# Stick-breaking attention: scores kept instead of computed twice

## The chip, the cores and the metric

The kernel runs on one core of a Trainium2 chip. The metric is the device time of one execution in microseconds. Before the change the median of three runs is 3508.5 us (3507.38 to 3514.27).

## The reference

The program is a two-block network on 512 tokens with 1024 features. The first block has two layers. Each layer projects the normalised input, runs five attention branches, gates and merges them. The change touches one of these branches, stick-breaking attention, with 4 heads of 64:

```
z = einsum('bqhd,bshd->bhqs', q, k) * scale            # scores
strict = s < t                                         # key strictly before the query
log_keep = where(strict, log_sigmoid(-z), 0)
later = cumsum(log_keep, keys, reverse=True) - log_keep
a = where(strict, exp(log_sigmoid(z) + later), 0)
out = einsum('bhqs,bshd->bqhd', a, v)
```

Since log_sigmoid(z) = z + log_sigmoid(-z), the exponent is z plus the inclusive suffix sum of log_keep. That is how both kernels compute it.

## The kernel before

**Layout.** Keys lie on partitions, queries on the free axis. For a head, key block b (128 keys) meets only the queries from block b on, so the four tiles of a head have 512, 384, 256 and 128 columns. A matmul in plain fp32 appears in the trace as two MATMUL instructions.

**Work for one head, `sb_tensor`, `sb_scalar` and `sb_vector` (lines 1655 to 1805).** `scores(hd)` on TensorE writes the four score tiles into PSUM. `negated(hd)` on VectorE copies them with the sign turned into `lk` (line 1769) and writes -|z| into `wt` (line 1773). `logs(hd)` on ScalarE replaces `wt` by log(1 + exp(wt)) (lines 1731 and 1734). `kept(hd)` on VectorE makes log_sigmoid(-z) from both in `lk` (line 1781) and multiplies its diagonal 128 columns by a 0/1 mask (line 1785). `weights(hd)` on TensorE builds the exponent in a PSUM bank: the score product again, the additive mask on the diagonal block (an identity product with `before_add`), a triangular product `from_here` for the suffix sum inside the block, and products with ones for the later blocks. `weights(hd)` on ScalarE takes the exponential from PSUM into `wt` (line 1742). `weigh(hd)` on TensorE multiplies by the values, and `gated(hd)` on VectorE multiplies the output by its gate (line 1793).

**Order.** Each engine runs its instructions in the order in which they are written; semaphores join the engines. On TensorE a round is `scores(hd + 1)`, filler, `weights(hd)`, filler, `weigh(hd)`. I call these filler A and filler B. On VectorE it was `negated(hd + 1)`, `kept(hd + 1)`, two filler items, `gated(hd)`. Two sets of `lk` and `wt` alternate between heads; one lies in an arena called `arena_even` in the trace, the other in `merged`.

**Filler.** In this branch the filler is the computation of the adaptive-norm modulations for the second block (`ada_tensor`, line 841). Each item on TensorE first claims one of two spare PSUM banks for `ada_columns` and turns the row of the item before it into columns (line 852, two columns wide), and then multiplies four streamed weight chunks by the conditioning (line 867). A claim waits until the former owner of the bank is drained. The columns always take the same one of the two banks, so an item's claim waits for VectorE's write of the columns of the item before (`ada_vector`, line 899, output `mods`). ScalarE copies the row (line 886).

**Elsewhere.** All projections use a high and a low part of the weights (lines 318 to 320). The weights stream from HBM in chunks of 512 KB through five slots on SyncE's queue.

Of the kernel before, what the change touches and what calls it, by code (L numbers as in the profile page):

```python
# [11 lines left out]
ALU = mybir.AluOpType  # L12
ACT = mybir.ActivationFunctionType
# [300 lines left out]
def mm(g, out, a, b, start, stop):  # L314
    pe = g.pe
    if not isinstance(a, Split):
        return pe.matmul(out, a, b, start=start, stop=stop)  # L317
    pe.matmul(out, a.high, b.high, start=start, stop=False)  # L318
    pe.matmul(out, a.high, b.low, start=False, stop=False)  # L319
    return pe.matmul(out, a.low, b.high, start=False, stop=stop)  # L320
# [1334 lines left out]
def sb_tensor(g, l, turn, opening):  # L1655

    pe, S, t, h = g.pe, g.event, g.t.sb, g.t.h
    key = lambda *a: ("sb", l) + a
    for j in range(2):
        for n in "qk":  # L1660
            project(g, key(n, j), turn, COL["sb_" + n][j * P:(j + 1) * P], (l,), h)
        if j == 0:
            fill_tensor(g)
    values_tensor(g, key("v"), turn, COL["sb_v"], (l,), h)
    ready = [S("zeroed").at("queries"), S("drained").at(key("v"))]
    ready += [S("drained").at(key(n, j)) for n in "qk" for j in range(2)]

    def scores(hd):
        j = hd // 2
        for b in range(QT):  # L1670
            i = g.claim(key("z", hd, b), turn.next(1))
            for m in g.after(pe, *ready):
                pe.wait_ge(*m)
            mm(g, g.banks(i)[:, 0:SEQ - b * P], t.k[:, j, b * P:(b + 1) * P], t.q[:, hd, b * P:SEQ], True,
               True).then_inc(*S("scored").up(pe, key(hd, b)))

    def weights(hd):
        j, lk = hd // 2, t.lk[hd % 2]
        for b in range(QT):
            n = SEQ - b * P  # L1680
            bank = g.banks(g.claim(key("w", hd, b), turn.next(1)))
            mm(g, bank[:, 0:n], t.k[:, j, b * P:(b + 1) * P], t.q[:, hd, b * P:SEQ], True, False)
            mm(g, bank[:, 0:P], g.ident, g.c.before_add, False, False)
            for m in g.after(pe, S("kept").at((l, hd))):
                pe.wait_ge(*m)
            done = mm(g, bank[:, 0:n], g.c.from_here, lk[b], False, b == QT - 1)
            for b2 in range(b + 1, QT):
                done = mm(g, bank[:, (b2 - b) * P:n], g.ones, lk[b2], False, b2 == QT - 1)
            done.then_inc(*S("scored").up(pe, key("w", hd, b)))

    def weigh(hd):
        wt = t.wt[hd % 2]
        i = g.claim(key("o", hd), turn.next(1))
        for m in g.after(pe, S("drained").at(key("w", hd, QT - 1))):
            pe.wait_ge(*m)
        for q in range(QT):
            for b in range(q + 1):
                done = mm(g, g.banks(i)[:, q * HD:(q + 1) * HD], wt[b][:, (q - b) * P:(q - b + 1) * P],
                          t.v[:, b, hd * HD:(hd + 1) * HD], b == 0, b == q)
        done.then_inc(*S("weighed").up(pe, key(hd)))  # L1700

    scores(0)
    fill_tensor(g)
    for hd in range(HEADS):
        if hd + 1 < HEADS:
            scores(hd + 1)
        fill_tensor(g)
        weights(hd)
        fill_tensor(g)
        weigh(hd)  # L1710


def sb_scalar(g, l, opening):
    act, S, t = g.act, g.event, g.t.sb
    key = lambda *a: ("sb", l) + a
    for j in range(2):
        g.weights.round(key("q", j))
        pair_scalar(g, key("q", j), pair_of(t.q, j), SCALE)
        g.weights.round(key("k", j))
        if j == 0:  # L1720
            fill_scalar(g)
    g.weights.round(key("v"))
    copy_scalar(g, key("v"), t.v[:, :, :].rearrange("p t c -> p (t c)"), g.bank(key("v"), 2))
    act.preload_act_table_set("natural_log_exp_and_others")

    def logs(hd):
        wt = t.wt[hd % 2]
        for b in range(QT):
            for m in g.after(act, S("stick").at((l, hd, b))):
                act.wait_ge(*m)  # L1730
            act.activation(wt[b], wt[b], ACT.Exp).then_inc(*S("stick_exp").up(act))
            for m in g.after(act):
                act.wait_ge(*m)
            act.activation(wt[b], wt[b], ACT.Ln, bias=1.0).then_inc(*S("stick_log").up(act, (l, hd, b)))

    def weights(hd):
        wt = t.wt[hd % 2]
        for b in range(QT):
            k = key("w", hd, b)
            for m in g.after(act, S("scored").at(k), S("kept").at((l, hd))):  # L1740
                act.wait_ge(*m)
            act.activation(wt[b], g.bank(k)[:, 0:SEQ - b * P], ACT.Exp).then_inc(*S("drained").up(act, k))

    logs(0)
    fill_scalar(g)
    for hd in range(HEADS):
        if hd + 1 < HEADS:
            logs(hd + 1)
        fill_scalar(g)
        weights(hd)  # L1750
        fill_scalar(g)


def sb_vector(g, l, opening):
    dve, S, t = g.dve, g.event, g.t.sb
    key = lambda *a: ("sb", l) + a
    for j in range(2):
        pair_vector(g, key("k", j), t.k[:, j, :])
        if j == 0:
            fill_vector(g)  # L1760

    def negated(hd):
        lk, wt = t.lk[hd % 2], t.wt[hd % 2]
        before = [S("weighed").at(key(hd - 2))] if hd > 1 else []
        for b in range(QT):
            k = key("z", hd, b)
            for m in g.after(dve, S("scored").at(key(hd, b)), *before):
                dve.wait_ge(*m)
            dve.tensor_scalar(lk[b], g.bank(k)[:, 0:SEQ - b * P], -1.0, None, ALU.mult).then_inc(
                *S("drained").up(dve, k))  # L1770
            for m in g.after(dve):
                dve.wait_ge(*m)
            dve.scalar_tensor_tensor(wt[b], lk[b], -1.0, lk[b], ALU.mult, ALU.min).then_inc(
                *S("stick").up(dve, (l, hd, b)))

    def kept(hd):
        lk, wt = t.lk[hd % 2], t.wt[hd % 2]
        for b in range(QT):
            for m in g.after(dve, S("stick_log").at((l, hd, b))):
                dve.wait_ge(*m)  # L1780
            dve.scalar_tensor_tensor(lk[b], lk[b], 0.0, wt[b], ALU.min, ALU.subtract).then_inc(
                *S("stick").up(dve))
            for m in g.after(dve):
                dve.wait_ge(*m)
            dve.tensor_tensor(lk[b][:, 0:P], lk[b][:, 0:P], g.c.before01, ALU.mult).then_inc(
                *S("kept").up(dve, (l, hd) if b == QT - 1 else None))

    def gated(hd):
        k = key("o", hd)
        y = g.t.gate[:, 2, :].rearrange("p (t c) -> p t c", t=QT)[:, :, hd * HD:(hd + 1) * HD]  # L1790
        for m in g.after(dve, S("weighed").at(key(hd))):
            dve.wait_ge(*m)
        dve.tensor_tensor(y, g.bank(k)[:, 0:QT * HD].rearrange("p (t c) -> p t c", t=QT), y, ALU.mult).then_inc(
            *S("drained").up(dve, k))

    negated(0)
    kept(0)
    fill_vector(g)
    for hd in range(HEADS):
        if hd + 1 < HEADS:  # L1800
            negated(hd + 1)
            kept(hd + 1)
        fill_vector(g, 2)
        gated(hd)
# [2513 lines left out]
def pack_constants():  # L4318
# [9 lines left out]
    causal[:, SEQ - P:] = np.where(j <= i, 0.0, NEG)  # L4328
    at["causal"] = first.const(causal)

    at["before01"] = first.const((i < j) * 1.0)
    at["before_add"] = first.const(np.where(i < j, 0.0, NEG))
    at["from_here"] = first.const((i >= j) * 1.0)

# [87 lines left out]
def name_constants(at, common, first):  # L4422
    c, s = Names(), Names()
    c.causal = first[:, at["causal"]:at["causal"] + SEQ]
    sq = lambda t, n: t[:, at[n]:at[n] + P]
    c.before01, c.before_add, c.from_here = (sq(first, n) for n in ("before01", "before_add", "from_here"))
    c.perm64, c.perm32 = sq(first, "perm64"), sq(first, "perm32")
    col = lambda t, n, w=1: t[:, at[n]:at[n] + w]
    c.inv64, c.inv32, c.sign64, c.sign32 = (col(first, n) for n in ("inv64", "inv32", "sign64", "sign32"))
# [31 lines left out]
def tiles(of, **more):  # L4461
    return namedtuple("Tiles", list(of) + list(more))(*of.values(), *more.values())


def layout_first(g, at, t_common, first, st):
# [35 lines left out]
        with ExitStack() as s2:  # L4501
            t.merged_split = g.pair("merged", [P, KT, SEQ], s2)
    heads = [("k", [P, 2, SEQ]), ("v", [P, QT, BR])]
    pieces = [(f"{n}{b}", [P, SEQ - b * P]) for n in ("lk", "wt") for b in range(QT)]
    of = carve(even, heads + pieces)
    sets = (of, carve(t.merged[:, :, :].rearrange("p k n -> p (k n)"), pieces))
    t.sb = tiles(of, q=t.q_even, lk=[[o[f"lk{b}"] for b in range(QT)] for o in sets], wt=[[o[f"wt{b}"] for b in range(QT)] for o in sets])
    of = carve(odd, heads + [("c_kv", [P, 1, SEQ]), ("c_n", [P, 1, SEQ]), ("qi", [P, SEQ]), ("ki", [P, SEQ]),
                                ("work", [P, 2, SEQ])] + [(f"drop{i}", [P, (i + 1) * P]) for i in range(1, QT - 1)])
    t.dsa = tiles(of, q=t.q_odd, drop=[None] + [of[f"drop{i}"] for i in range(1, QT - 1)] + [of["c_n"][:, 0, :]])  # L4510
# [245 lines left out]
```

## Time and profile before

| what | value |
|---|---|
| median of three runs | 3508.5 us |
| profiled execution, own time | 3506.41 us |
| its span | 3505.1 us |
| TensorE busy | 3292.2 us, 94% |
| VectorE busy | 1721.1 us, 49% |
| ScalarE busy | 1313.9 us, 37% |
| mean granted TensorE clock | 0.973 of full |

Rows name engines as PE (TensorE matmul), PEld (its weight load), DVE (VectorE), ACT (ScalarE), POOL (GpSimd), SP (SyncE). The granted clock is given in parts of full speed; it has two levels, 1.0 and 0.5. A stretch with a value between them spent part of its time at each. In a row of the timeline, matmuls that overlap are merged, so the time that one of them takes from the next is the difference of two starts. A bracket at the end of a row is the idle time of the engine before it and who ended it.

### The profile page before, as it was taken

What the parts mean: (1) busy time and instruction counts of PE and PEld (TensorE: products, weight loads), DVE (VectorE), ACT (ScalarE), POOL (GpSimd) and SP (SyncE); (2) the same over time, 40 slices, a digit from 0 to 9 for tenths busy, and PEclk for the clock granted to TensorE, in tenths of its full rate; (3) what the DMA queues carried; (4) which work ended last, traced back from release to release, by engine and by line L of the source; (5) the groups of instructions that cost most, each with busy time, mean ns of one, the idle gap of its engine ahead of it and who ended that gap; (6) DMA issues with size and microseconds to landing.
All of it is one profiled execution on the core that took longest, in us unless ns stands there. A gap on an engine that the chain in (4) does not pass through costs nothing.

```text
span 3505.1 us, 44707 instructions
## 1 busy us (share of the span) xinstructions
PE 3292.2 (94%) x17128; PEld 2630.5 (75%) x17128; DVE 1721.1 (49%) x3172; ACT 1313.9 (37%) x2278; POOL 1056.1 (30%) x513
## 2 busy tenths in 40 slices
PE   8999999999999998999898899999999988889999
PEld 6677777777867776777786677888988556668877
DVE  5348345423138635532798655222565655543234
ACT  4333334333333333333423433222443455533332
POOL 3123122234303222124336432232553000034443
PEclk9999899999999999999999999999999999999999
DMA  5532121132562122124222001122332100022222
GB/s 183 182 136 81 40 81 65 53 101 99 180 221 77 47 70 84 41 70 141 67 67 67 1 31 61 61 67 67 112 117 82 40 35 1 4 71 91 99 96 79
DMA packets 87479, 286.41 MB, mean 82 GB/s; under 512 B 9697, under 2 KB 20321, under 8 KB 86497
## 3 DMA queue, kind: packets, MB, share of 16 engines
q1 hardware_dynamic: 85968, 272.67, 22.9%
q10 hardware_dynamic: 1296, 10.88, 0.8%
q8 instruction: 135, 2.21, 0.3%
q14 instruction: 80, 0.65, 0.1%
HBM read 279.32 MB, written 4.19 MB: 81 GB/s over the span
## 4 chain that ended last, share of the span: by engine, by line
PE 54%; DVE 7%; ACT 3%; issue 2%; POOL 0%; DMA 0%; DVEq 0%; ACTq 0%; POOLq 0%
PE psum L318 14%; PE psum L319 14%; PE psum L320 14%; PE psum L317 9%; PE psum L3768 1%; DVE mla_cols L3857 1%; PE psum L3756 1%; PE psum L1192 1%; DVE padded L2806 0%; DVE h_low L582 0%; DVE ml_weights L3209 0%; PE psum L3734 0%; DVE squares L511 0%; ACT weights_high L395 0%; ACT mla_probs L3813 0%
## 5 line engine op out<-in xcount | busy, mean ns | idle before, releaser
L413 POOL TENSOR_TENSOR weights_low<-weights_loaded,weights_high 128x1024 fp32r<-128x1024 f32 (+3 forms) x456 | 958.6, 2102 | 2362.7 <-ACT weights_high L395 2277.6
L318 PE MATMUL psum<-h_high,weights_high 128*128 128x512 f32 (+1 forms) x2384 | 900.4, 378 | 45.5 <-DVE h_low L582 21.2
L319 PE MATMUL psum<-h_low,weights_high 128*128 128x512 f32 (+1 forms) x2384 | 882.6, 370 | 0.0
L320 PE MATMUL psum<-h_high,weights_low 128*128 128x512 f32 (+1 forms) x2384 | 881.7, 370 | 0.0
L395 ACT CAST weights_high<-weights_loaded 128x1024 fp32r<-128x1024 f32 (+3 forms) x456 | 422.0, 926 | 472.7 <-PE psum L320 398.3
L318 PEld LDWEIGHTS psum<-h_high,weights_high 128*128 128x128 f32 x2384 | 456.1, 191 | 134.4 <-issue 35.7
L319 PEld LDWEIGHTS psum<-h_low,weights_high 128*128 128x128 f32 x2384 | 455.7, 191 | 77.4 <-issue 4.1
L320 PEld LDWEIGHTS psum<-h_high,weights_low 128*128 128x128 f32 x2384 | 454.6, 191 | 76.6
L318 PE MATMUL psum<-act_high,weights_high 128*128 128x512 f32 (+1 forms) x528 | 187.7, 355 | 8.2 <-DVE act_low L4155 6.2
L319 PE MATMUL psum<-act_low,weights_high 128*128 128x512 f32 (+1 forms) x528 | 187.5, 355 | 0.0
L320 PE MATMUL psum<-act_high,weights_low 128*128 128x512 f32 (+1 forms) x528 | 187.4, 355 | 0.0
L4155 DVE TENSOR_TENSOR act_low<-ffn_act,act_high 128x512 fp32r<-128x512 f32 (+1 forms) x66 | 127.7, 1934 | 109.2 <-ACT act_high L4116 108.7
L4015 DVE TENSOR_SCALAR psum<-ffn_row,second 128x770 f32<-128x770 f32 (+1 forms) x44 | 41.7, 949 | 280.7 <-ACT ffn_row L3987 280.7
L922 ACT ACTIVATE sig<-psum 128x512 f32<-128x512 f32 x80 | 47.9, 598 | 316.2 <-PE psum L320 305.1
L318 PE MATMUL psum<-weights_high,h_high 128*128 128x512 f32 (+2 forms) x368 | 125.2, 340 | 10.4 <-DVE h_low L580 5.2
L1262 ACT ACTIVATE x<-x,softmax_cols 128x256 f32<-128x256 f32 (+4 forms) x192 | 98.8, 515 | 86.0 <-DVE softmax_cols L1296 81.2
L319 PE MATMUL psum<-weights_low,h_high 128*128 128x512 f32 (+2 forms) x368 | 123.7, 336 | 0.0
L320 PE MATMUL psum<-weights_high,h_low 128*128 128x512 f32 (+2 forms) x368 | 123.6, 336 | 0.0
L953 DVE SCALAR_TENSOR_TENSOR sig<-sig,psum 128x512 f32<-128x512 f32 x64 | 44.0, 687 | 161.7 <-PE psum L320 159.0
L318 PEld LDWEIGHTS psum<-act_high,weights_high 128*128 128x128 f32 x528 | 100.3, 190 | 23.3 <-issue 5.8
L2769 DVE SCALAR_TENSOR_TENSOR psum<-padded,second,psum 128x256 f32<-128x256 f32 (+1 forms) x180 | 112.1, 623 | 6.4
L1288 DVE CUSTOM_DVE_ANT_0 x<-psum,first 128x256 f32<-128x256 f32 (+4 forms) x168 | 69.2, 412 | 87.8 <-PE psum L317 82.8
(506 smaller groups left out, 5307.9 us busy)
## 6 DMA issues: line engine op xcount, KB each, us to landing
weights_loaded<-stream_dram SPq DMA_DIRECT2D x468, 512.0 KB, 3.3
weights_loaded<-stream_dram SPq DMA_DIRECT2D x80, 128.0 KB, 2.3
weights_loaded<-stream_dram SPq DMA_DIRECT2D x24, 384.0 KB, 3.0
weights_loaded<-stream_dram SPq DMA_DIRECT2D x8, 272.0 KB, 4.9
x<-x_dram SPq DMA_DIRECT2D x4, 512.0 KB, 6.6
arena_mem<-mem_dram ACTq DMA_DIRECT2D x2, 1024.0 KB, 4.9
x<-x_dram ACTq DMA_DIRECT2D x1, 2048.0 KB, 9.1
x_kept_dram<-x ACTq DMA_DIRECT2D x1, 2048.0 KB, 9.6
```

The source lines that it names most:

```text
L317: return pe.matmul(out, a, b, start=start, stop=stop)
L318: pe.matmul(out, a.high, b.high, start=start, stop=False)
L319: pe.matmul(out, a.high, b.low, start=False, stop=False)
L320: return pe.matmul(out, a.low, b.high, start=False, stop=stop)
L395: act.copy(self.high[t % NSPLIT][:, 0:size], self.raw[c % NRAW][:, 0:size]).then_inc(*g.event("weights_high").up(act, c))
L413: pool.tensor_tensor(self.low[s][:, 0:size], raw[:, 0:size], self.high[s][:, 0:size], ALU.subtract).then_inc(*g.event("weights_low").up(po ...
L922: act.activation(g.t.sig[g.sigs.place[key]][:, :], g.bank(key), ACT.Tanh, scale=0.5).then_inc(*S("drained").up(act, key))
L953: dve.scalar_tensor_tensor(dst, s[:, :], 1.0, g.bank(key), ALU.add, ALU.mult).then_inc(*S("drained").up(dve, key))
L1262: act.activation(p[:, h, 0:u.keys], p[:, h, 0:u.keys], ACT.Exp, bias=c[:, 4 + h:5 + h], scale=SCALE, accum_out=None if u.keep is not None ...
L1288: dve.tensor_tensor_reduce(p[:, h, 0:u.keys], g.bank(("logits", u.key, h))[:, 0:u.keys], u.mask, 1.0, LOWEST, ALU.add, ALU.max, c[:, h:h + ...
L2769: dve.scalar_tensor_tensor(acc, t.up[:, c, at + j:at + j + size], cw[:, j:j + 1], acc, ALU.mult, ALU.add).then_inc(*S("convolved").up(dve, ...
L4155: dve.tensor_tensor(t.ffn[l].part[i % NPART].low[:, 0:n], t.ffn[l].act[:, f, lo - lo0:lo - lo0 + n], t.ffn[l].part[i % NPART].high[:, 0:n] ...
```

## The change

The negated scores are kept in SBUF in a tile of their own (`neg`), instead of being overwritten. In `negated` the additive mask is subtracted from the diagonal 128 columns, so both later steps see masked scores. `kept` writes its result to `wt` and no longer multiplies by the 0/1 mask. TensorE's `weights` is left with the suffix sums only. A new step `scored` on VectorE subtracts `neg` from the sums, out of PSUM into `wt`, and ScalarE takes the exponential in place in SBUF. VectorE's order in a round is now `negated(hd + 1)`, `scored(hd)`, `kept(hd + 1)`, two filler items, `gated(hd)`. The constant `before01` goes.

```diff
     def weights(hd):
-        j, lk = hd // 2, t.lk[hd % 2]
+        keep = t.wt[hd % 2]
         for b in range(QT):
             n = SEQ - b * P
             bank = g.banks(g.claim(key("w", hd, b), turn.next(1)))
-            mm(g, bank[:, 0:n], t.k[:, j, b * P:(b + 1) * P], t.q[:, hd, b * P:SEQ], True, False)
-            mm(g, bank[:, 0:P], g.ident, g.c.before_add, False, False)
             for m in g.after(pe, S("kept").at((l, hd))):
                 pe.wait_ge(*m)
-            done = mm(g, bank[:, 0:n], g.c.from_here, lk[b], False, b == QT - 1)
+            done = mm(g, bank[:, 0:n], g.c.from_here, keep[b], True, b == QT - 1)
             for b2 in range(b + 1, QT):
-                done = mm(g, bank[:, (b2 - b) * P:n], g.ones, lk[b2], False, b2 == QT - 1)
+                done = mm(g, bank[:, (b2 - b) * P:n], g.ones, keep[b2], False, b2 == QT - 1)
             done.then_inc(*S("scored").up(pe, key("w", hd, b)))
...
-        for m in g.after(pe, S("drained").at(key("w", hd, QT - 1))):
+        for m in g.after(pe, S("stick_weight").at((l, hd))):
...
-            k = key("w", hd, b)
-            for m in g.after(act, S("scored").at(k), S("kept").at((l, hd))):
+            for m in g.after(act, S("drained").at(key("w", hd, b))):
                 act.wait_ge(*m)
-            act.activation(wt[b], g.bank(k)[:, 0:SEQ - b * P], ACT.Exp).then_inc(*S("drained").up(act, k))
+            act.activation(wt[b], wt[b], ACT.Exp).then_inc(*S("stick_weight").up(act, (l, hd) if b == QT - 1 else None))
...
-            dve.tensor_scalar(lk[b], g.bank(k)[:, 0:SEQ - b * P], -1.0, None, ALU.mult).then_inc(
+            dve.tensor_scalar(neg[b], g.bank(k)[:, 0:SEQ - b * P], -1.0, None, ALU.mult).then_inc(
                 *S("drained").up(dve, k))
             for m in g.after(dve):
                 dve.wait_ge(*m)
-            dve.scalar_tensor_tensor(wt[b], lk[b], -1.0, lk[b], ALU.mult, ALU.min).then_inc(
+            dve.tensor_tensor(neg[b][:, 0:P], neg[b][:, 0:P], g.c.before_add, ALU.subtract).then_inc(*S("stick").up(dve))
+            for m in g.after(dve):
+                dve.wait_ge(*m)
+            dve.scalar_tensor_tensor(wt[b], neg[b], -1.0, neg[b], ALU.mult, ALU.min).then_inc(
                 *S("stick").up(dve, (l, hd, b)))
...
-            dve.scalar_tensor_tensor(lk[b], lk[b], 0.0, wt[b], ALU.min, ALU.subtract).then_inc(
-                *S("stick").up(dve))
-            for m in g.after(dve):
+            dve.scalar_tensor_tensor(wt[b], neg[b], 0.0, wt[b], ALU.min, ALU.subtract).then_inc(
+                *S("kept").up(dve, (l, hd) if b == QT - 1 else None))
+
+    def scored(hd):
+        neg, wt = t.neg[hd % 2], t.wt[hd % 2]
+        for b in range(QT):
+            k = key("w", hd, b)
+            for m in g.after(dve, S("scored").at(k)):
                 dve.wait_ge(*m)
-            dve.tensor_tensor(lk[b][:, 0:P], lk[b][:, 0:P], g.c.before01, ALU.mult).then_inc(
-                *S("kept").up(dve, (l, hd) if b == QT - 1 else None))
+            dve.tensor_tensor(wt[b], g.bank(k)[:, 0:SEQ - b * P], neg[b], ALU.subtract).then_inc(*S("drained").up(dve, k))
...
         if hd + 1 < HEADS:
             negated(hd + 1)
+        scored(hd)
+        if hd + 1 < HEADS:
             kept(hd + 1)
         fill_vector(g, 2)
         gated(hd)
```

## Rows read from the trace of the kernel before

**Rows 1.** The page: busy time, granted clock in 40 slices, last chain.

```profile
PE 3292.2 (94%) x17128; PEld 2630.5 (75%) x17128; DVE 1721.1 (49%) x3172; ACT 1313.9 (37%) x2278; POOL 1056.1 (30%) x513
...
PEclk9999899999999999999999999999999999999999
...
PE 54%; DVE 7%; ACT 3%; issue 2%; POOL 0%; DMA 0%; DVEq 0%; ACTq 0%; POOLq 0%
```

**Rows 2.** Busy time of each engine in the two stick-breaking stretches, clock, DMA.

```profile
124.30:202.70 78.40, 74.43 (x473) 49.16 (x474) 31.03 (x76) 30.10 (x59) 2.36 (x1) 1.00 0.61 224
967.00:1045.90 78.90, 74.98 (x473) 49.06 (x473) 31.03 (x76) 30.05 (x59) 2.36 (x1) 1.00 0.62 223
```

**Rows 3.** Waits of TensorE from 124.3 to 202.7: us, times, longest.

```profile
PE psum L852 <- DVE mods L899: 1.6, 1, 1.6
```

**Rows 4.** Timeline of TensorE, a round of the second head: start, us, what.

```profile
150.00 2.38 PE L317 MATMUL psum<-queries_even,arena_even 128*128 128x512 f32 x8
...
155.10 1.12 PE L317 MATMUL psum<-queries_even,arena_even 128*128 128x512 f32 x2
156.06 0.39 PE L317 MATMUL psum<-first,common 128*128 128x128 f32 x2
156.28 1.02 PE L317 MATMUL psum<-merged,first 128*128 128x512 f32 x2
157.15 1.46 PE L317 MATMUL psum<-merged,common 128*128 128x384 f32 x6
158.44 0.81 PE L317 MATMUL psum<-queries_even,arena_even 128*128 128x384 f32 x2
159.09 0.38 PE L317 MATMUL psum<-first,common 128*128 128x128 f32 x2
...
160.61 0.60 PE L317 MATMUL psum<-queries_even,arena_even 128*128 128x256 f32 x2
161.04 0.38 PE L317 MATMUL psum<-first,common 128*128 128x128 f32 x2
...
161.92 0.39 PE L317 MATMUL psum<-queries_even,arena_even 128*128 128x128 f32 x2
162.14 0.39 PE L317 MATMUL psum<-first,common 128*128 128x128 f32 x2
...
162.59 0.95 PE L852 MATMUL psum<-first,ada_row 128*128 128x2 f32 x8
```

**Rows 5.** Timeline of VectorE in the same round.

```profile
151.19 0.69 DVE L1769 TENSOR_SCALAR arena_even<-psum 128x512 f32<-128x512 f32 x1 [0.49 <-PE psum L317]
...
155.39 0.69 DVE L1781 SCALAR_TENSOR_TENSOR arena_even<-arena_even 128x512 f32<-128x512 f32 x1
156.11 0.29 DVE L1785 TENSOR_TENSOR arena_even<-arena_even,first 128x128 f32<-128x128 f32 x1
156.44 0.56 DVE L1781 SCALAR_TENSOR_TENSOR arena_even<-arena_even 128x384 f32<-128x384 f32 x1
...
158.79 0.17 DVE L899 SCALAR_TENSOR_TENSOR mods<-psum,common 128x8 f32<-128x8 f32 x1
```

**Rows 6.** Timeline of TensorE: filler A of the first head, last head.

```profile
134.53 1.05 PE L852 MATMUL psum<-first,ada_row 128*128 128x2 f32 x8 [1.65 <-DVE mods L899]
...
190.02 1.13 PE L317 MATMUL psum<-queries_even,arena_even 128*128 128x512 f32 x2
...
197.51 0.95 PE L852 MATMUL psum<-first,ada_row 128*128 128x2 f32 x8
```

**Rows 7.** Windows of 10 us from the start of idle stretches, columns as rows 2.

```profile
545.70:555.70 10.00, 7.38 (x37) 5.61 (x37) 7.25 (x31) 5.21 (x13) 0.73 (x1) 1.00 0.01 2
...
734.00:744.00 10.00, 7.42 (x23) 5.89 (x23) 1.23 (x1) 2.06 (x2) 2.37 (x1) 0.66 0.76 271
1227.30:1237.30 10.00, 7.42 (x28) 6.04 (x28) 1.22 (x1) 2.48 (x4) 3.10 (x2) 0.83 0.20 67
...
3379.50:3389.50 10.00, 7.30 (x33) 6.09 (x33) 4.62 (x4) 4.35 (x6) 4.70 (x3) 1.00 0.31 105
```

More of the change, by code:

```diff
@@ L1762, in negated @@
     def negated(hd):
-        lk, wt = t.lk[hd % 2], t.wt[hd % 2]
+        neg, wt = t.neg[hd % 2], t.wt[hd % 2]
         before = [S("weighed").at(key(hd - 2))] if hd > 1 else []
@@ L1772, in negated @@
                 dve.wait_ge(*m)
-            dve.scalar_tensor_tensor(wt[b], lk[b], -1.0, lk[b], ALU.mult, ALU.min).then_inc(
+            dve.tensor_tensor(neg[b][:, 0:P], neg[b][:, 0:P], g.c.before_add, ALU.subtract).then_inc(*S("stick").up(dve))
+            for m in g.after(dve):
+                dve.wait_ge(*m)
+            dve.scalar_tensor_tensor(wt[b], neg[b], -1.0, neg[b], ALU.mult, ALU.min).then_inc(
                 *S("stick").up(dve, (l, hd, b)))
     def kept(hd):
-        lk, wt = t.lk[hd % 2], t.wt[hd % 2]
+        neg, wt = t.neg[hd % 2], t.wt[hd % 2]
         for b in range(QT):
@@ L1780, in kept @@
                 dve.wait_ge(*m)
-            dve.scalar_tensor_tensor(lk[b], lk[b], 0.0, wt[b], ALU.min, ALU.subtract).then_inc(
-                *S("stick").up(dve))
-            for m in g.after(dve):
+            dve.scalar_tensor_tensor(wt[b], neg[b], 0.0, wt[b], ALU.min, ALU.subtract).then_inc(
+                *S("kept").up(dve, (l, hd) if b == QT - 1 else None))
+    def scored(hd):
+        neg, wt = t.neg[hd % 2], t.wt[hd % 2]
+        for b in range(QT):
+            k = key("w", hd, b)
+            for m in g.after(dve, S("scored").at(k)):
                 dve.wait_ge(*m)
-            dve.tensor_tensor(lk[b][:, 0:P], lk[b][:, 0:P], g.c.before01, ALU.mult).then_inc(
-                *S("kept").up(dve, (l, hd) if b == QT - 1 else None))
+            dve.tensor_tensor(wt[b], g.bank(k)[:, 0:SEQ - b * P], neg[b], ALU.subtract).then_inc(*S("drained").up(dve, k))
     def gated(hd):
@@ L4329, in pack_constants @@
     at["causal"] = first.const(causal)
-    at["before01"] = first.const((i < j) * 1.0)
     at["before_add"] = first.const(np.where(i < j, 0.0, NEG))
@@ L4425, in name_constants @@
     sq = lambda t, n: t[:, at[n]:at[n] + P]
-    c.before01, c.before_add, c.from_here = (sq(first, n) for n in ("before01", "before_add", "from_here"))
+    c.before_add, c.from_here = (sq(first, n) for n in ("before_add", "from_here"))
     c.perm64, c.perm32 = sq(first, "perm64"), sq(first, "perm32")
@@ L4503, in layout_first @@
     heads = [("k", [P, 2, SEQ]), ("v", [P, QT, BR])]
-    pieces = [(f"{n}{b}", [P, SEQ - b * P]) for n in ("lk", "wt") for b in range(QT)]
+    pieces = [(f"{n}{b}", [P, SEQ - b * P]) for n in ("neg", "wt") for b in range(QT)]
     of = carve(even, heads + pieces)
     sets = (of, carve(t.merged[:, :, :].rearrange("p k n -> p (k n)"), pieces))
-    t.sb = tiles(of, q=t.q_even, lk=[[o[f"lk{b}"] for b in range(QT)] for o in sets], wt=[[o[f"wt{b}"] for b in range(QT)] for o in sets])
+    t.sb = tiles(of, q=t.q_even, **{n: [[o[f"{n}{b}"] for b in range(QT)] for o in sets] for n in ("neg", "wt")})
     of = carve(odd, heads + [("c_kv", [P, 1, SEQ]), ("c_n", [P, 1, SEQ]), ("qi", [P, SEQ]), ("ki", [P, SEQ]),
```

## The prediction

> **What bounds the kernel now.** I read the page first: TensorE is busy for 3292.2 us of a 3505.1 us span, and the chain that ended last is mostly TensorE's work [rows 1]. So a matmul taken away is worth its time, unless TensorE must then wait for something that was hidden before. Which of the two holds is not to be read from a share of the whole span, so I went to the two stretches in which stick-breaking runs, one in each layer. They last 78.4 and 78.9 us; TensorE is busy for 74.4 and 75.0 of these, VectorE for 31.0, ScalarE for some 30, and the granted clock is 1.00 in both [rows 2]. TensorE's longest wait there is one of 1.6 us, and the one it waits for is VectorE's `mods` (line 899) [rows 3]. This is the row to keep in mind: a small write that the filler work (the adaptive-norm steps) needs, standing in VectorE's queue behind the work for the heads. Last I read one head's round on both engines in order of time.
>
> **A round before.** TensorE starts the next head's scores at 150.00, then filler A, then this head's `weights` at 155.10, then filler B at 162.59, then `weigh` [rows 4]. VectorE does `negated` of the next head from 151.19 to 155.39, `kept` from 155.39 to 158.79, and then the `mods` write that belongs to filler A [rows 5]. Filler B begins by claiming the same PSUM bank that this write drains. It is ready at 158.79 + 0.17 and wanted at 162.59: 3.6 us to spare.
>
> **What goes from TensorE.** Per head, in `weights`: four second score products, from start to next start 0.96, 0.65, 0.43 and 0.22, and four mask products of 0.22 each [rows 4]. That is 2.26 + 0.88 = 3.14 us. Of the first one 0.09 stays, because the first matmul behind a filler starts that much late whichever it is (0.96 against 0.87 for the 512-column product at 156.28). So 3.05 us a head, 24.4 us over 4 heads and 2 layers. `weights` shrinks from 7.49 to 4.43 us.
>
> **What comes to VectorE.** (a) The mask subtraction on 128 columns in `negated` is like the mask multiplication that leaves `kept` (0.33 from start to start, 156.11 to 156.44 [rows 5]): 1.3 us move from `kept` into `negated`, which becomes 5.5 us; `kept` becomes 2.1. (b) The new step `scored`, a subtraction from PSUM over 512, 384, 256 and 128 columns. Its nearest row is the negation from PSUM of the same tiles: with the second op of equal sizes, `negated` takes 4.20 for two such passes [rows 5], so one pass is 2.10 us, in pieces of 0.72, 0.59, 0.46 and 0.33. Bounds: a pass twice as dear, 4.2 us, would end 1.5 us later in each head (from its start at 157.67 below: 161.87 in place of 160.41), 11.7 us over eight heads; nothing speaks for a cheaper one. I take 2.10, since the row reads the same bank at the same widths. ScalarE's exponentials keep their sizes and only read from another place; they end before filler B begins in either order, so they are put at nothing.
>
> **Where the new step stands decides the result.** On VectorE the order is now `negated` (next head), `scored` (this head), `kept` (next head), then the two `mods` writes. So the write that filler B's bank waits for stands behind `scored`, and `scored` waits for the last sum of this head's `weights`. Put on the clock of the round shown: `negated` runs 151.19 to 156.69. The first sum is all issued at 155.10 + 2.25 = 157.35; a reader started 0.32 after the last issue when VectorE took the first scores (150.00 + 0.87, read at 151.19). So `scored` begins its pieces at 157.67, 158.97 and 159.62; the last follows at 160.08 and ends at 160.41. `kept` then ends at 162.51, `mods` at 162.68, and TensorE starts filler B 0.06 later, at 162.74. Before, it started at 162.59. TensorE has been free since 155.10 + 4.43 = 159.53. The whole 3.05 us turns into a wait of some 3.2 us at the head of filler B, and the round ends 0.15 us later than now. Behind the waiting instruction stand the filler and `weigh`, whose input is ready by then but can't pass. This is so for the first three heads. For the first head `kept` of head 0 waits for ScalarE's logarithms and ends where it did, so the wait of 1.65 us at 134.53 [rows 6] stays.
>
> The last head has no next one. There only `scored` stands in front of `mods`: it ends 160.41 - 155.10 = 5.31 us after `weights` begins, so filler B starts at 190.02 + 5.31 + 0.23 = 195.56 in place of 197.51 [rows 6], 1.95 us earlier. Its weights come in chunks whose slots are freed by filler A before 190.0, so I expect no new wait for the stream. Behind it the next branch starts on TensorE's own chain, and everything moves up together.
>
> Sum of the steps: 3 x 0.15 - 1.95 = -1.5 us a layer, -3.0 us in all.
>
> **What the new idle does to the clock.** There are six new idle stretches of about 3 us, in places where TensorE had none and the clock was 1.00. What does such a stretch do in this trace? I looked at twelve of its idle stretches of 2.4 to 3.1 us, each in a window of 10 us from about its beginning, in which TensorE is busy for 6.7 to 7.6 us (four shown [rows 7]). Two stayed at 1.00, six show 0.83 and four 0.66, that is 3.4 and 6.8 us at the lower of the two levels (1.2 in place of 2.4 GHz). The mean is (6 x 3.4 + 4 x 6.8) / 12 = 4.0 us at the lower level; half of it, 2.0 us, is lost if TensorE is busy all that time. Some of the low time lies in the idle itself, so I take 1.6 us for each of the six, between 0 and 3.4: 9.6 us.
>
> The Trainium skill (TensorE: Matmul & The Clock Gate, "Loop structure matters more than you think") says that VectorE copying a result out of PSUM doesn't cool the engine, while a wait between all matmuls does; its table under "Why this matters for your kernels" advises against idle gaps between bursts. The trace agrees with the second: ten of the twelve stretches were followed by the lower level. By the first alone the clock term would be 0 and the sum -3.0 us.
>
> **Sum.** -3.0 + 9.6 = +6.6 us. The profiled execution took 3506.4 us (span 3505.1), which gives 3513.0; the median of the runs shown is 3508.5, 2.1 above it, which gives 3515.1. I say 3514.
>
> **Rivals.**
> - The clock holds. For it: two of twelve stretches left it at 1.00, and there is dense work on both sides. Against it: the other ten. Then only the steps count: 3508.5 - 3.0 = 3505.5 us.
> - TensorE gets its time back. If the `mods` write did not stand between (for instance if filler B claimed another bank), the saving would be 24.4 us and the time 3484. For it: TensorE is busy for 95% of these stretches. Against it: the one wait for that write at 134.53 shows that the filler does wait for it, in just this way.
> - Clearly slower: the clock falls at each of the six stretches and stays low for 6.8 us of full work, 3.4 us lost each. 6 x 3.4 - 3.0 = +17.4, 3526 us. For it: four of twelve windows read 0.66. Against it: six read 0.83, and part of the low time would lie in the idle. It decides over 0.2% as soon as a stretch costs more than 1.7 us on average.
>
> **How the numbers follow.** Chances: forecast 0.66, its own range 3508 to 3521; the clock holds 0.20; full saving 0.06; far side 0.08. The range of 8 in 10 takes in the case in which the clock holds and most of the way to the far side: 3502 to 3524. A difference of 0.2%, 7 us, is about what a measurement of this kernel can tell. The forecast lies right at this bound, so its 0.66 is split nearly evenly, 0.33 slower and 0.33 same; the clock holding is mostly same (0.13, and 0.07 faster); with full saving and the far side: faster 0.14, same 0.45, slower 0.41.
>
> **What would show it.** In the changed kernel: TensorE's busy time in each stretch lower by some 12 us while the stretch is as long or longer; three waits of 3 us a layer, before line 852's matmul, for VectorE's `mods`, and a short one in the last head; `scored` beginning right behind the last sum, at 2.1 us a head; the granted clock below 1.00 in both stretches. If the waits of 3 us are missing, the step on VectorE's order is wrong. If they are there and the clock is 1.00, only the clock term is wrong. If the time falls by 20 us, the whole argument is.

## The result and the profile after

The changed kernel takes 3522.61 us (median of 10 runs, 3518.93 to 3534.24); the kernel before, run beside it, 3504.16 us (median of 10). The ratio is 1.0051, 95% interval 1.0039 to 1.0063: slower by 18 us, between 14 and 22. The time lies in the forecast range (3502 to 3524). The forecast's own step from the kernel before was +6.6 us, so the loss is nearly three times what its sum gave, and the time lies outside the range that the forecast case had for itself (3508 to 3521). The forecast also started from 3508.5 us, the median of three runs; the median of ten is 4.3 us lower. Laid on 3504.2 us the range would be some 3498 to 3520, and the result would lie above it.

The profiled execution is the slowest of the ten: 3534.24 us, span 3532.9, against 3505.1 before. First the two stick-breaking stretches, from the first score to the first matmul of the next branch (columns as in rows 2):

```profile
125.26:219.57 94.31, 82.33 (x409) 50.62 (x409) 38.93 (x92) 29.37 (x58) 2.36 (x1) 0.78 0.50 185
981.87:1072.35 90.48, 78.66 (x408) 49.30 (x408) 38.98 (x93) 29.49 (x59) 2.34 (x1) 0.81 0.53 196
```

Taken between the same two events, the stretches lasted 77.0 and 77.8 us before. They grew by 17.3 and 12.7 us, 30 us together, a little more than the whole span did (27.8). In this execution all of the loss is here. TensorE has 64 fewer matmul records in each ([rows 2]: 473) and is still busy for longer, because the granted clock is 0.78 and 0.81 in place of 1.00.

The waits of TensorE in the first stretch, from 124 to 220 (us in all, times, longest):

```profile
PE psum L852 <- DVE mods L899: 11.5, 5, 3.0
PE psum L317 <- ACT arena_even L694: 1.3, 1, 1.3
```

In [rows 3] the first of these was 1.6 us, once. Now a round of the second head, first on TensorE, as in [rows 4]:

```profile
164.64 1.12 PE L317 MATMUL psum<-merged,first 128*128 128x512 f32 x2
165.60 1.46 PE L317 MATMUL psum<-merged,common 128*128 128x384 f32 x6
...
168.86 0.39 PE L317 MATMUL psum<-merged,first 128*128 128x128 f32 x2
172.24 1.75 PE L852 MATMUL psum<-first,ada_row 128*128 128x2 f32 x8 [2.99 <-DVE mods L899]
```

then on VectorE, as in [rows 5]:

```profile
159.42 0.69 DVE L1766 TENSOR_SCALAR arena_even<-psum 128x512 f32<-128x512 f32 x1 [1.39 <-PE psum L317]
...
167.18 0.69 DVE L1790 TENSOR_TENSOR merged<-psum,merged 128x512 f32<-128x512 f32 x1 [2.27 <-PE psum L317]
168.47 1.41 DVE L1790 TENSOR_TENSOR merged<-psum,merged 128x384 f32<-128x384 f32 x3 [0.60 <-PE psum L317]
169.91 2.07 DVE L1781 SCALAR_TENSOR_TENSOR arena_even<-arena_even 128x512 f32<-128x512 f32 x4
172.01 0.17 DVE L899 SCALAR_TENSOR_TENSOR mods<-psum,common 128x8 f32<-128x8 f32 x1
```

Read the two together. `weights` begins at 164.64 and its last sum starts at 168.86. VectorE follows the sums (`scored`, line 1790), then does `kept` of the next head (2.07), then the small `mods` write. TensorE's filler B starts 0.23 after that write starts, 7.60 us after `weights` began. In between it stood idle for 2.99 us. The row of filler B also shows the price: its eight two-column matmuls take 1.75 us, where they took 0.95 in [rows 4].

Last, windows of 16 us from the beginning of each of the six waits:

```profile
145.00:161.00 16.00, 13.00 (x51) 8.26 (x51) 4.86 (x12) 1.74 (x4) 0.00 (x0) 0.61 0.36 132
169.20:185.20 16.00, 13.01 (x50) 8.33 (x50) 4.57 (x12) 1.76 (x4) 0.00 (x0) 0.60 0.44 165
193.40:209.40 16.00, 12.56 (x70) 7.01 (x70) 3.38 (x9) 2.03 (x5) 0.00 (x0) 0.79 0.54 194
1000.00:1016.00 16.00, 12.90 (x59) 9.02 (x59) 6.12 (x15) 2.81 (x6) 0.00 (x0) 0.68 0.47 165
1022.70:1038.70 16.00, 13.01 (x50) 8.36 (x50) 4.44 (x12) 1.72 (x4) 0.00 (x0) 0.59 0.44 164
1046.90:1062.90 16.00, 13.01 (x73) 7.51 (x73) 3.35 (x9) 2.33 (x5) 0.00 (x0) 0.79 0.55 208
```

A clock of 0.61 over 16 us is 2 x 0.39 x 16 = 12.5 us at the lower level. The six come to 12.5, 12.8, 6.7, 10.2, 13.1 and 6.7 us, 10.3 on average, where the prediction had taken 4.0 from [rows 7]. The length of the window is not the reason: read over 16 us too, the twelve stretches of the prediction still give 4.0.

By the same reckoning the two stretches together hold 76 us at the lower level. The six waits don't account for all of it. Some 10 us lie behind the wait of 1.65 us in filler A of the first head, which the kernel before has as well. First the changed kernel, one layer each, then the kernel before at the same two places:

```profile
132.60:142.60 10.00, 8.34 (x33) 3.79 (x33) 6.62 (x17) 5.02 (x11) 0.00 (x0) 0.66 0.76 282
989.20:999.20 10.00, 8.35 (x41) 4.47 (x41) 7.31 (x18) 5.54 (x12) 0.00 (x0) 0.83 0.73 263
```

```profile
132.80:142.80 10.00, 8.35 (x46) 4.96 (x46) 8.73 (x23) 4.98 (x11) 0.00 (x0) 1.00 0.76 281
975.40:985.40 10.00, 8.35 (x43) 4.56 (x43) 8.70 (x22) 4.95 (x10) 0.00 (x0) 1.00 0.82 272
```

These figures come from the execution with the lowest mean clock of the ten (0.964; the other nine have 0.966 to 0.968). An estimate from these clocks, 2 x 0.002 x 3520, is that another execution had some 14 us less at the lower level, so 10.3 us a wait is more than usual.

### The profile page after: what moved, and what is told of

Its sections match the earlier page's. It is cut to its first block, busy times and chain, and to the rows that moved or that the text cites. A ratio compares the mean times of both kernels' runs of the same rounds, so it can differ in the third digit from the quotient of the medians.

```text
span 3532.9 us, 44515 instructions
## 1 busy us (share of the span) xinstructions
PE 3303.0 (93%) x17000; PEld 2630.8 (74%) x17000; DVE 1735.9 (49%) x3204; ACT 1312.8 (37%) x2278; POOL 1056.0 (30%) x513
## 4 chain that ended last, share of the span: by engine, by line
PE 53%; DVE 7%; ACT 3%; issue 2%; POOL 0%; DMA 0%; DVEq 0%; ACTq 0%; POOLq 0%
PE psum L318 14%; PE psum L319 14%; PE psum L320 14%; PE psum L317 9%; PE psum L3774 1%; DVE mla_cols L3863 1%; PE psum L3762 1%; PE psum L1192 1%; DVE padded L2812 0%; DVE h_low L582 0%; PE psum L3740 0%; DVE ml_weights L3215 0%; DVE squares L511 0%; ACT weights_high L395 0%; ACT mla_probs L3819 0%
```

## The experiments

Each edit is against the changed kernel unless it says otherwise. Intervals are of the ratio to the kernel before.

**1. `early_write`: one filler item of VectorE ahead of `scored`.**

```diff
             negated(hd + 1)
+        fill_vector(g)
         scored(hd)
         if hd + 1 < HEADS:
             kept(hd + 1)
-        fill_vector(g, 2)
+        fill_vector(g)
         gated(hd)
```

> The changed kernel with one filler item of VectorE moved ahead of `scored`: `negated` (next head), the `mods` write, `scored`, `kept`, the other write. Theory (the loss comes from the write that filler B's bank waits for, standing behind `scored` and `kept`, and from the clock that falls in the idle): the write is done about 1.8 us after `weights` begins, TensorE is free at 4.4, so the waits of 3 us are gone, the clock reads 1.00 in both stretches, and the 24 us of removed products come back: about 3482 us, some 22 below the kernel before, up to 3 us less if the weight stream becomes late. Rival 1 (the weight stream bounds these stretches once the round is shorter): a wait for DMA in place of the one for VectorE, 3494 or more. Rival 2 (VectorE's added work itself is what costs): no better than 3515.

Measured: 3484.58 us (median of 5), ratio 0.9946 (0.9933 to 0.9960). TensorE in its first stretch, and the two stretches:

```profile
PE psum L852 <- DVE mods L899: 1.6, 1, 1.6
PE psum L317 <- ACT arena_even L694: 1.3, 1, 1.3
PE psum L867 <- DMA weights_loaded<-stream_dram: 1.0, 1, 1.0
```

```profile
125.16:192.18 67.02, 64.41 (x408) 40.13 (x409) 38.91 (x92) 29.37 (x58) 2.35 (x1) 0.97 0.70 260
959.78:1027.85 68.07, 64.82 (x409) 40.37 (x409) 39.33 (x93) 31.13 (x60) 2.36 (x2) 0.97 0.74 269
```

The new waits are gone, and what is left is the wait of 1.6 us that stood there before. The same arithmetic on the same engines, with one tiny write in another place, is 38 us faster than the changed kernel and 20 us faster than the kernel before. VectorE is as busy as after the change (38.9 us), so its added work costs nothing that shows where it stands in nobody's way; experiment 3, without that work, is no faster (3486.57 us). Rival 1 is out as the bound of these stretches: the stream moves 260 to 269 GB/s in place of 223, and its one wait of 1.0 us stood there before too (1.1 us). It shows only in small. One row of the filler takes 2.74 us, with the clock at 1.00, where most take 1.92:

```profile
165.80 2.74 PE L867 MATMUL psum<-weights_loaded,silu_c 128*32 128x512 f32 x16
```

The clock is 0.97 and not the 1.00 that was expected; that is some 4 us at the lower level in each stretch, at most 2 us lost in each. Such things are why 20 us came back and not 24.

**2. `work_in_wait`: TensorE computes the removed products again, while it would wait.**

```diff
...
+    def idle_work(hd):
+        j, bank = hd // 2, g.banks(g.claim(key("o", hd), turn.next(1)))
+        for b in range(QT):
+            mm(g, bank[:, 0:SEQ - b * P], t.k[:, j, b * P:(b + 1) * P], t.q[:, hd, b * P:SEQ], True, True)
+            mm(g, bank[:, 0:P], g.ident, g.c.before_add, True, True)
...
         weights(hd)
+        idle_work(hd)
         fill_tensor(g)
         weigh(hd)
```

> The changed kernel with useless work in TensorE's idle stretch: behind the last sum of each head the four score products and four mask products are computed again, into the bank of the output, where nothing reads them. TensorE does what it did before the change, but in the place where it would wait; VectorE's work and order are those of the changed kernel. Theory (clock): no wait above 1 us at filler B, the clock 1.00 in both stretches, the time that of the kernel before or 1 to 3 us off it, so near 3504, while the changed kernel takes 3522. Rival (the extra time comes from VectorE's longer work or from the wait as such, not from the clock): it stays at 3515 to 3522.

Measured: 3509.62 us (median of 11), ratio 1.0012 (1.0004 to 1.0021). The two stretches:

```profile
126.17:202.91 76.74, 74.86 (x473) 49.05 (x473) 38.89 (x92) 29.38 (x58) 2.37 (x1) 1.00 0.62 228
965.92:1043.60 77.68, 74.64 (x472) 48.99 (x473) 38.91 (x92) 29.49 (x58) 2.36 (x1) 1.00 0.61 226
```

This separates the wait from the clock. VectorE does all that it does in the changed kernel, and filler B starts no earlier (in the round of the second head 7.60 us after `weights`, as in the changed kernel), but TensorE is not idle and the clock stays at 1.00. Useless matmuls make the kernel 13 us faster. All eleven runs have a mean clock of 0.971 to 0.975, the kernel before 0.968 to 0.976, the changed kernel 0.964 to 0.968, so this doesn't rest on one profile. The stretches are 0.3 and 0.2 us shorter than before. The median, however, is 4.6 us above the kernel before where 1 to 3 us on either side were expected; these 4.6 us are not in the stretches of the profiled execution (3504.15 us, one of the fastest of its runs), and where they are stays open.

**3. `products_out`: TensorE's part alone, on the kernel before.** The second score products and the mask products are left out, so the exponent lacks the score and the mask.

```diff
-            mm(g, bank[:, 0:n], t.k[:, j, b * P:(b + 1) * P], t.q[:, hd, b * P:SEQ], True, False)
-            mm(g, bank[:, 0:P], g.ident, g.c.before_add, False, False)
...
-            done = mm(g, bank[:, 0:n], g.c.from_here, lk[b], False, b == QT - 1)
+            done = mm(g, bank[:, 0:n], g.c.from_here, lk[b], True, b == QT - 1)
```

> The kernel before with only TensorE's part of the change: the second score products and the mask products are left out, so the exponent lacks the score and the mask; VectorE and ScalarE are untouched. Theory: the `mods` write is done 3.9 us after `weights` begins and TensorE is free at 4.4, so nothing waits and 24 us are saved: 3480 us. Rival (removed products are worth little here since something else ends the round, as the weight stream): 3495 or more.

Measured: 3486.57 us (median of 5), ratio 0.9947 (0.9934 to 0.9961), so 18 us of the expected 24. `weights` shrinks as computed (4.44 us in the second head, 152.76 to 157.20). The rest is partly in small waits (0.4 us for `mods` in each stretch, 0.6 and 0.5 for the low weights, where the kernel before shows neither) and in streamed weights that come later: the filler's weight products from 165.55 to 169.05 take 3.50 us, where the kernel before took 1.86. So the rival is out, though the stream takes a small part back. The removed products are worth most of their time where TensorE needn't wait for the write.

**4. `kept_first`: `kept` of the next head ahead of `scored`, both writes behind.**

```diff
             negated(hd + 1)
-        scored(hd)
-        if hd + 1 < HEADS:
             kept(hd + 1)
+        scored(hd)
         fill_vector(g, 2)
```

> The changed kernel with `kept` of the next head ahead of `scored` on VectorE; both writes stay behind. `scored` is then done about 5.8 us after `weights` begins and the write at 6.0, TensorE is free at 4.4: idle stretches of about 1.5 us in place of 3.0. Theory: 1.4 us of the 3.05 are gained in each of eight heads, 11 to 12 us, if the clock holds: 3492 with the clock at 1.00. If the clock falls after 1.5 us of idle as after 3 us, 3505 to 3520. Rival (the place of the write does not matter): as the changed kernel, 3522.

Measured: 3504.32 us (median of 11), ratio 0.9995 (0.9984 to 1.0005): no difference from the kernel before. The two stretches, and TensorE's waits in the first:

```profile
124.10:202.10 78.00, 69.55 (x408) 43.92 (x409) 38.91 (x92) 29.36 (x58) 2.35 (x1) 0.91 0.61 225
968.23:1041.71 73.48, 65.62 (x409) 40.47 (x409) 38.90 (x92) 29.48 (x58) 2.36 (x1) 0.95 0.65 238
```

```profile
PE psum L852 <- DVE mods L899: 7.5, 5, 2.5
```

The waits fell from 11.5 to 7.5 us, and the clock was 0.91 and 0.95, higher than the 0.78 and 0.81 of the changed kernel, but not 1.00. So the time came out just below the 3505 to 3520 expected for a clock that falls, 12 us above the 3492 for one that holds. The waits are not all 1.5 us: the first of each layer is 2.5 and 2.6, where VectorE works without a gap up to the write (in the first layer from 130.81 to 143.00). These two are alike on TensorE, and yet the one was followed by 12.8 us of 16 at the lower level, and the other by none:

```profile
140.50:156.50 16.00, 13.52 (x53) 8.63 (x53) 4.89 (x12) 2.70 (x6) 0.00 (x0) 0.60 0.48 182
984.70:1000.70 16.00, 13.40 (x89) 8.61 (x89) 9.46 (x23) 6.81 (x14) 0.00 (x0) 1.00 0.67 241
```


**5. `products_back`: VectorE's part alone.** The products are computed again at their old places, and each sum then starts over them.

```diff
...
+            mm(g, bank[:, 0:n], t.k[:, j, b * P:(b + 1) * P], t.q[:, hd, b * P:SEQ], True, True)
+            mm(g, bank[:, 0:P], g.ident, g.c.before_add, True, True)
             for m in g.after(pe, S("kept").at((l, hd))):
                 pe.wait_ge(*m)
             done = mm(g, bank[:, 0:n], g.c.from_here, keep[b], True, b == QT - 1)
```

> The changed kernel with TensorE's removed products put back at their old places inside `weights` (each sum then starts over them, so they have no effect). This is VectorE's part of the change alone. Theory (a wait is made by the place of the write, whatever TensorE does): `weights` takes 7.5 us again, `scored` ends 0.65 behind it, the write 2.3 later; filler B waits 3 us as in the changed kernel, and each round is 3 us longer than before: 3 x 3.0 + 0.9 = 9.9 us a layer, 20 us, and with low clocks of 20 us as in the changed kernel about 3545. Rival (with more work on TensorE the wait is covered): near the kernel before, 3505 to 3510.

Measured: 3549.10 us (median of 4), ratio 1.0126 (1.0109 to 1.0143). TensorE's waits in the first stretch, and both stretches:

```profile
PE psum L852 <- DVE mods L899: 10.6, 5, 2.8
```

```profile
124.95:221.17 96.22, 85.64 (x473) 53.43 (x473) 38.89 (x92) 29.38 (x58) 2.36 (x1) 0.88 0.51 182
984.27:1086.81 102.54, 91.83 (x473) 58.63 (x473) 38.90 (x92) 29.48 (x58) 2.36 (x1) 0.82 0.46 172
```

More work on TensorE doesn't cover the wait, since `scored` follows TensorE's last sum wherever that is. Only work behind the sum, as in experiment 2, covers it. The theory holds (about 3545 expected). The low spans behind its six long waits differ widely, though the same narrow filler stands behind each. The first and the fifth of the six, from the start of the wait:

```profile
147.70:163.70 16.00, 13.24 (x82) 7.54 (x82) 7.87 (x20) 4.23 (x9) 0.00 (x0) 0.89 0.43 156
1029.20:1045.20 16.00, 13.24 (x51) 8.51 (x51) 4.46 (x11) 1.28 (x3) 0.00 (x0) 0.59 0.36 134
```

That is 3.5 and 13.1 us at the lower level; the six windows give 8.3 on average.

**6. `all_early`: `early_write`, and the same for the first head.** The edit holds that of experiment 1 and besides:

```diff
     negated(0)
-    kept(0)
     fill_vector(g)
+    kept(0)
```

> `early_write` with, besides, the filler item of VectorE that stands behind `kept` of the first head moved ahead of it. This is to take away the last wait for a `mods` write, 1.65 us in each layer, which the kernel before has as well. Theory: no wait of TensorE for VectorE's `mods` is left in either stretch, the time is 3 us below `early_write`'s 3484.6, more if the lower clock of 3.4 us that followed this wait goes too: 3478 to 3482. Rival (another wait stands right behind it): 3484 to 3486.

Measured: 3485.09 us (median of 6), ratio 0.9937 (0.9920 to 0.9953), no different from `early_write` within the noise. The 3478 to 3482 us of the theory were missed at the median, and the rival's 3484 to 3486 were met. The six runs spread from 3478.3 to 3488.4 us, however, so a gain of 3 us can't be told from none. What the trace shows is that the rival's mechanism is there: in the place of the 1.6 us for `mods`, filler A of the first head now waits 0.8 us for another write, ScalarE's copy of the row.

```profile
PE psum L852 <- ACT ada_row L886: 0.8, 1, 0.8
```

**7 and 8. `dense_behind_wait` and `plain_behind_wait2`: useless dense work right behind the wait.** It stands behind the claim at the head of filler B, for the first three heads.

```diff
...
+    def dense_work(hd):
+        bank = g.bank(key("o", hd))
+        for i in range(14):
+            pe.matmul(bank[:, 0:SEQ], h.high[:, i % KT, 0:P], h.high[:, i % KT, :], start=True, stop=True)
...
+        g.claim(key("o", hd), turn.next(1))
+        if hd + 1 < HEADS:
+            g.between = lambda: dense_work(hd)
         fill_tensor(g)
```

(`ada_tensor` calls `g.between` right behind its claim) and in the second one

```diff
-        for i in range(14):
-            pe.matmul(bank[:, 0:SEQ], h.high[:, i % KT, 0:P], h.high[:, i % KT, :], start=True, stop=True)
+        for i in range(4):
+            pe.matmul(bank[:, 0:SEQ], t.k[:, i % 2, 0:P], t.q[:, i, :], start=True, stop=True)
```

> The changed kernel with 14 useless products of 512 columns in the split format, back to back, right behind the wait at the head of filler B, for the first three heads (output bank, overwritten later). They last 3.2 us at full clock. The question is why the lower clock lasts 7 to 14 us behind these waits and 3 to 7 us behind the idle stretches that the prediction looked at, which are followed by such products. Theory (what follows the idle decides how fast the clock returns): low spans of 3 to 7 us here, in place of 10 to 14. Rival (the length comes from the idle stretch or from its neighbours): 10 to 14 us as in the changed kernel. The time itself grows by the added products, 19 us at full clock and up to 38 at the lower one, and says nothing.

> As `dense_behind_wait`, but the useless work behind each of the six waits is 4 products of 512 columns in plain fp32 (3.5 us at full clock) in place of 14 in the split format (3.2 us). The low spans behind the wait were 7 to 14 us in the changed kernel and 3 to 7 us with the split-format products. Theory A (plain fp32 products bring the clock back more slowly than the split ones): 10 to 14 us again, 3535 to 3545. Theory B (any dense work of 512 columns does, and it is the narrow matmuls of the filler and of `weigh` that are slow to bring it back): 3 to 7 us, near 3530.

Measured: 3529.26 us (median of 2) and 3529.34 us (median of 3), ratios 1.0067 (1.0043 to 1.0092) and 1.0073 (1.0037 to 1.0109). Windows of 16 us from the start of the waits, as above for the changed kernel; first `dense_behind_wait` (the first, the lowest, the last of six), then `plain_behind_wait2`:

```profile
140.70:156.70 16.00, 12.94 (x78) 9.73 (x82) 5.31 (x13) 1.97 (x5) 0.00 (x0) 0.89 0.45 170
...
997.50:1013.50 16.00, 12.92 (x63) 9.40 (x64) 3.78 (x10) 1.60 (x4) 0.00 (x0) 0.79 0.30 114
...
1043.60:1059.60 16.00, 12.73 (x78) 8.74 (x78) 3.29 (x9) 1.68 (x4) 0.00 (x0) 0.89 0.41 155
```

```profile
141.60:157.60 16.00, 12.91 (x81) 7.89 (x84) 6.36 (x15) 3.14 (x7) 0.00 (x0) 1.00 0.51 192
...
994.40:1010.40 16.00, 12.94 (x68) 7.99 (x68) 4.88 (x13) 1.58 (x4) 0.00 (x0) 0.89 0.37 140
...
1040.10:1056.10 16.00, 11.95 (x77) 6.64 (x76) 3.39 (x9) 1.77 (x4) 0.00 (x0) 1.00 0.46 177
```

The waits are as long as in the changed kernel (3.1 us), yet the six windows hold 4.6 us at the lower level on average with the split-format products and 1.8 with the plain ones, in place of 10.3. Theory A finds no support; theory B fits, if anything too well, since three of six waits were followed by no fall at all. These windows are one execution each, and experiments 4 and 5 show how much the low spans differ within one. But the mean clock of the whole execution points the same way in every run: 0.969 and 0.971 with the split-format products, 0.969 to 0.973 with the plain ones, 0.964 to 0.968 in the changed kernel. The added work is 19 to 21 us at full clock and cost only 7 us over the changed kernel (give or take some 10 us, by the intervals); the rest came back through the clock. That plain products bring it back better than split-format ones is not shown by two and three runs.

## Why the prediction came out as it did

- **What TensorE saves.** Right. `weights` is issued in 4.4 us in place of 7.5, and in `products_out` the saving shows (18 us of 24). One sign named for it didn't come: TensorE's busy time in a stretch was to fall by some 12 us and rose from 74.4 to 82.3, because matmuls at the lower clock count as busy for longer. In `early_write`, at a clock of 0.97, it is 64.4, 10 us less.
- **What VectorE gains in work.** Right: 38.9 us in place of 31.0 in a stretch, 7.9 more, against 4 x 2.1 = 8.4 with the gaps between instructions; the four new subtractions of a head have the durations taken for them (0.69 for 512 columns).
- **The write behind `scored`.** Right, nearly to the digit. Filler B was put 7.64 us after the start of `weights` (162.74 - 155.10); it starts after 7.60. In the last head it was put after 5.54 us; it starts after 5.49 (208.99 to 214.48). Experiments 1, 2 and 5 show it as the cause: moving the write ends the waits, and giving TensorE its products back doesn't.
- **The stream.** Right, no new wait of weight for it: 0.45 us once in the first stretch.
- **The clock.** Right in kind, wrong in size, and this is the term that was mis-sized. Six new idle stretches were priced at 1.6 us each, 9.6 in all, from 4.0 us at the lower level. They had 10.3 us. The prediction took off 0.4 of the 2.0 us for low time that lies in the idle itself; here the clock fell about when the idle ended or later, and TensorE was busy through the low time. It also let the wait of 1.65 us in the first head stay at no price, and there some 10 us at the lower level came in this execution. In the profiled execution the stretches without any clock term would last 77.0 - 1.5 and 77.8 - 1.5 us; they last 94.3 and 90.5, which leaves 33 us for the clock, over 76 us at the lower level. At the medians it is 18.4 + 3.0 = 21 us, in place of 9.6. If all of it is laid on the six waits it is 3.6 us for each: just above the 3.4 that the far side rival took as the most. Experiment 2 shows that it is the clock and not the wait, since the clock at 1.00 brings the time back to within 5 us of before.
- **Why it was mis-sized.** Eight of the twelve stretches behind [rows 7] are followed by split-format products of 256 or 512 columns; filler B and `weigh` are narrow (2 columns, 32 output rows, 64 columns). Experiments 7 and 8 put dense work in that place and the low spans shrink to the length that the prediction had read. So the rows were read rightly and, it seems, carried over to a place that is not like theirs. This is in part argued. The four of the twelve that other products follow, plain ones of 128 or 129 columns first, read 0, 3.4, 3.4 and 3.4 us, less than the eight (4.7 on average), so few columns alone don't make a low span long. And behind the same filler, after waits of 2.5 to 2.9 us, it was anything from none to 13 us (experiments 4 and 5). What decides a single case stays open; six priced at one mean was too firm.
- **The rivals.** "The clock holds" is out. "Full saving" is what `early_write` reaches, to 20 of 24 us, under the condition that the rival named: the filler's write no longer stands in the way. The far side (+17.4 us, given 0.08) is close to what happened (+18.4), by the mechanism that it names. That the time still lies in the range of 8 in 10 is luck in part: the start was 4.3 us too high, and this made up for some of the clock term.

## What to carry to other kernels

When work moves from the engine that bounds the kernel to one with idle time, list what stands behind the new step in that engine's queue, and who waits for each, down to the writes of 0.2 us. A step that has to follow the bounding engine's last result should stand behind everything that the bounding engine needs next: here one line moved turned 18 us lost into 20 us gained. An idle stretch of TensorE is not priced by its own length alone but by the clock behind it. Here that differed with the work that came next, and from one wait to the next where the work was the same. So read it where the same work follows, take a range and not a mean, and don't expect one profile to show the usual case.

## What was not expected of the hardware

Behind idle stretches of the same 3.0 to 3.1 us, the granted clock was at its lower level for 10.3 us on average when narrow matmuls followed, for 4.6 us with 14 split-format products of 512 columns first, and for 1.8 us with 4 plain fp32 ones of 512 columns, in one execution each. TensorE counts as busy for 12.6 to 13.0 of 16 us in all of these windows but one (11.95), so its busy share doesn't tell them apart. In the changed kernel the clock stayed low for 13 us on end in which the profile shows no gap on TensorE. Here are the wait of the second head and what came behind it:

```profile
169.20:172.20 3.00, 0.04 (x1) 0.00 (x0) 2.78 (x7) 1.17 (x3) 0.00 (x0) 1.00 0.47 180
172.40:185.40 13.00, 13.00 (x50) 8.27 (x51) 1.99 (x5) 0.59 (x1) 0.00 (x0) 0.50 0.43 161
```

In the wait itself the granted clock was 1.00; it was at its lower level only when TensorE worked again. In `kept_first` two waits of 2.5 and 2.6 us with the same filler behind them were followed by 12.8 us at the lower level and by none.

Useless matmuls can pay for themselves: eight a head in a place where TensorE would wait made the changed kernel 13 us faster.
